# Two transformer blocks on one core: GpSimd instead of VectorE multiplies the banded attention's probabilities by the inverse sums

## The reference

```python
# 8 query heads of 64 in 2 groups of 4; blocks of 128 queries, each against its own and the previous 128 keys
scores = einsum('bnqhgd,bnkhd->bnhgqk', qb, kb) / sqrt(64)
scores = where(mask, scores, -inf)                 # distance in 0..127
m = maximum(max(scores), sink)
p = exp(scores - m)
denom = sum(p) + exp(sink - m)
out = einsum('bnhgqk,bnkhd->bnqhgd', p / denom, vb)
```

## Time and profile before

| | us |
|---|---|
| median of three runs | 2773.33 (2773.2 to 2775.22) |
| the profiled execution's own time | 2773.03 |
| its span, first to last instruction | 2771.2 |
| PE busy in the span | 2693.5 (97%) |
| DVE, ACT, POOL busy | 1417.8, 899.5, 1480.3 |
| the window part: first scores to first tile of the `w_out` product | 407.91 to 473.70 |

### The profile page before, as it was taken

The page is one execution under the profiler, slowest core; times in us unless marked ns, Lnnn a source line. Parts: engine busy times, 40 slices in busy tenths (PEclk is TensorE's granted clock), DMA queues, the critical chain, the costliest instruction groups (busy, mean ns, idle before and its releaser), DMA issues.

```text
span 2771.2 us, 34189 instructions
## 1 busy us (share of the span) xinstructions
PE 2693.5 (97%) x13446; PEld 2204.7 (80%) x13446; DVE 1417.8 (51%) x1911; ACT 899.5 (32%) x1418; POOL 1480.3 (53%) x1410
## 2 busy tenths in 40 slices
PE   7999997999999999999999999999997999999998
PEld 6989885878888888888797777878665888888887
DVE  4365638385554531835204444447678667665122
ACT  5354427242221220312113333325464222223032
POOL 3731310667777777875332221356224788786873
PEclk9999999999999999999999999999998999999999
DMA  6432330522222254435544232533021222226442
GB/s 215 167 122 84 114 120 11 182 89 65 91 92 85 83 205 175 151 92 111 120 112 94 83 111 81 190 116 107 31 76 46 76 86 81 92 77 228 152 150 101
DMA packets 184598, 309.40 MB, mean 112 GB/s; under 512 B 7044, under 2 KB 117999, under 8 KB 184439
## 3 DMA queue, kind: packets, MB, share of 16 engines
q1 hardware_dynamic: 137728, 214.45, 24.4%
q10 hardware_dynamic: 46711, 92.77, 9.5%
HBM read 232.18 MB, written 75.01 MB: 111 GB/s over the span
## 4 chain that ended last, share of the span: by engine, by line
PE 84%; DVE 9%; ACT 2%; issue 2%; POOL 2%; ACTq 0%; DMA 0%; DVEq 0%; POOLq 0%
PE PS L1039 27%; PE PS L291 20%; PE PS L1053 16%; PE PS L1724 4%; PE PS L2794 3%; PE PS L1730 2%; PE PS L1781 2%; PE PS L2428 2%; PE PS L2470 1%; PE PS L2498 1%; PE PS L2486 1%; DVE SC L658 1%; DVE XTf L1277 1%; DVE SC L2242 1%; POOL WL L3498 1%
## 5 line engine op out<-in xcount | busy, mean ns | idle before, releaser
L3494 POOL CAST WH<-raw 128x512 fp32r<-128x512 f32 (+1 forms) x240 | 180.3, 765 | 921.4 <-issue 734.3
L291 PE MATMUL PS<-UH,WH 128*128 128x512 f32 x1040 | 425.3, 409 | 8.6 <-DVE UL L739 3.7
L291 PE MATMUL PS<-UH,WL 128*128 128x512 f32 x1040 | 406.4, 391 | 0.0
L291 PE MATMUL PS<-UL,WH 128*128 128x512 f32 x1040 | 406.1, 391 | 0.0
L3498 POOL TENSOR_TENSOR WL<-raw,WH 128x512 fp32r<-128x512 f32 (+1 forms) x240 | 336.4, 1412 | 0.0
L1039 PE MATMUL PS<-UH,WH 128*128 128x512 f32 x640 | 251.4, 393 | 18.9 <-DVE SC L1307 11.3
L1593 POOL TENSOR_TENSOR WL<-raw,WH 128x512 fp32r<-128x512 f32 x176 | 259.9, 1486 | 0.0
L291 PEld LDWEIGHTS PS<-UH,WH 128*128 128x128 f32 x1040 | 195.5, 188 | 71.0 <-issue 19.8
L1039 PE MATMUL PS<-UL,WH 128*128 128x512 f32 x640 | 250.9, 392 | 0.0
L1039 PE MATMUL PS<-UH,WL 128*128 128x512 f32 x640 | 250.9, 392 | 0.0
L1558 POOL CAST WH<-WLf 128x512 fp32r<-128x512 f32 x152 | 140.4, 923 | 181.8 <-DVE WLf L1269 181.8
(11 more groups left out here) (400 smaller groups left out, 5900.7 us busy)
## 6 DMA issues: line engine op xcount, KB each, us to landing
raw<-in_w_down SPq DMA_DIRECT2D x44, 1024.0 KB, 5.7
raw<-in_w_up SPq DMA_DIRECT2D x33, 1024.0 KB, 5.1
raw<-in_w_in SPq DMA_DIRECT2D x27, 1024.0 KB, 9.8
act_rows<-SC SPq DMA_DIRECT2D x22, 1024.0 KB, 4.0
ULf<-act_rows SPq DMA_DIRECT2D x28, 512.0 KB, 3.4
raw<-in_w_gate SPq DMA_DIRECT2D x11, 1024.0 KB, 5.3
raw<-in_w_out SPq DMA_DIRECT2D x8, 1024.0 KB, 6.2
xres<-XTf ACTq DMA_DIRECT2D x16, 512.0 KB, 2.8
```

The costliest lines, as they stand in the source:

```text
L291: mm = pe.matmul(PS[:, banks[f], :], w[:, k, f * P:(f + 1) * P], u[:, k, half(h)], start=(k == 0 and j == 0), stop=(k == n_k - 1 and j == 2))
L3494: pool.tensor_copy(wh[slot][:, cols], raw[slot % 2][:, cols]).then_inc(hi_done[slot], 1)
```

## The change

The four multiplies of `divide(u)` leave DVE's queue and go to GpSimd's, in a new method `gpsimd` of the stage. GpSimd runs it for all 16 units, between the first and the second round of the segment `out1_a`. It waits for the reciprocal of the unit, multiplies, and raises a new semaphore `divided`. PE's `turn(u)` waits for that one. ACT's `probs(u)` waits, from the third unit on, until unit u - 2 is divided, since both use the same columns for their sums. What stays on DVE in `divide` is the addition and the reciprocal.

```diff
@@ setup @@
-                self.mx, self.inv, self.p_ready = c("attend_mx", 16), c("attend_inv", 32), c("attend_den", 32)
+                self.mx, self.inv, self.den_ready = c("attend_mx", 16), c("attend_inv", 32), c("attend_den", 16)
+                self.divided = c("first_divided", 16)
@@ PE, turn(u) @@
-                    pe.wait_ge(*self.p_ready(2 * u + 2))
+                    pe.wait_ge(*self.divided(u + 1))
@@ ACT, probs(u) @@
                     act.wait_ge(*self.m_ready(u + 1))
+                    if u >= 2:
+                        act.wait_ge(*self.divided(u - 1))
@@ First @@
+            def gpsimd(self, pool):
+
+                for u in range(16):
+                    nk, den = self.window_keys(u % 8)[1], self.columns(3, u)
+                    pool.wait_ge(*self.inv(2 * u + 3 if u < 15 else 32))
+                    for i in range(4):
+                        x = self.wP[u % 3][:, i * CH:i * CH + nk * P]
+                        d = pool.tensor_scalar(x, x, den[:, i:i + 1], None, ALU.mult)
+                    d.then_inc(self.divided.sem, 1)
@@ DVE, divide(u) @@
-                    nk = self.window_keys(u % 8)[1]
                     es, den = self.columns(2, u), self.columns(3, u)
                     dve.wait_ge(*self.e_done(u + 1))
-                    dve.tensor_tensor(den, den, es, ALU.add).then_inc(self.p_ready.sem, 1)
-                    dve.wait_ge(*self.p_ready(2 * u + 1))
+                    dve.tensor_tensor(den, den, es, ALU.add).then_inc(self.den_ready.sem, 1)
+                    dve.wait_ge(*self.den_ready(u + 1))
                     dve.reciprocal(den, den).then_inc(self.inv.sem, 1)
-                    dve.wait_ge(*self.inv(2 * u + 3 if u < 15 else 32))
-                    for i in range(4):
-                        x = self.wP[u % 3][:, i * CH:i * CH + nk * P]
-                        d = dve.tensor_scalar(x, x, den[:, i:i + 1], None, ALU.mult)
-                    d.then_inc(self.p_ready.sem, 1)
@@ GpSimd, the list of segments @@
                 body(0, first=True)
+                if seg == "out1_a":
+                    first.gpsimd(pool)
                 if iters > 1:
```

## The result

| | before | after |
|---|---|---|
| median, us | 2774.48 (2773.2 to 2776.11, 6 runs) | 2792.58 (2785.69 to 2794.05, 6 runs) |
| profiled execution, its span | 2773.03, 2771.2 | 2792.58, 2790.8 |
| first scores to first tile of the `w_out` product | 65.8 (407.9 to 473.7) | 83.4 (411.1 to 494.5) |
| from there to the end of the span | 2297.5 | 2296.3 |

The changed kernel is slower by 0.61% (ratio 1.0061, 95% interval 1.0048 to 1.0074), 18.1 us between the medians. The profiled spans differ by 19.6: 3.2 arise before the window part, 17.6 in it, and 1.2 are given back after it. The 3.2 are not put down to the change: the first scores began anywhere from 406.0 to 411.1 us in the fourteen profiles of this study, all of which run the same work up to there.

What follows compares the result with a forecast made beforehand. DVE was taken as the bound, ACT close second. 13 units at 3.35 us, plus 4.0 for ACT's copies, less 0.6, made 47.0 against 51.74; 4.8 - 0.7 - 0.5 = 3.6 gained, so 2769.7 us, range 2765.5 to 2778.5.

Steps and rivals of the forecast that it cites:

- What bounds the kernel now: Window part: PE waits 15.4 us for DVE's multiply; DVE sets 3.56 us per unit, ACT next with 3.26.
- What leaves DVE: DVE's queue: four multiplies, 1.06 us per full unit, leave; its pitch falls from 3.56 to about 2.4, ACT next.
- What GpSimd pays: GpSimd's queue: 0.40 us per 128 x 256 multiply, range 0.27 to 0.69; four take 1.60, so GpSimd is no bound.
- The loop of two units: Exponentials, reciprocal, multiplies, turn, copy, exponentials of unit u + 2: 6.70 us for two units, 3.35 each.
- 30 us for each microsecond on one multiply: Price sensitivity: 13 x 2 on the loop plus 4 on turn(1); the gain is gone from 0.52 us.
- its rival: GpSimd's multiply is dear: at 0.9 us each, 11.4 us worse, about 2785; chance beyond 0.70: 0.15.
- the sum: Turn(1) to turn(14): 47.0 us against 51.74, 4.8 less; minus 0.7 for a later turn(1) and 0.5 for contention: 3.6.
- The clock: PE's clock drops cost up to 1.3 and 1.0 us; without them and multiply at 0.35, gain 7.4; chance 0.25 over 5.5.
- Contention: DVE's five two-input operations beside GpSimd's multiplies each lose about 0.55 us, mostly hidden: minus 0.5 in all.
- Edits at no cost: ACT's new wait for unit u - 2 ends before it is reached; PE's wait only changes its releaser; renamed semaphores do nothing.
- The rival beyond 0.70 us: GpSimd's multiply costs over 0.70 us, making the kernel slower by more than 0.2%; chance 0.15.
- the prediction's own signs of being wrong: Four multiplies over 2.1 us, PE waiting over 15.4 us before turns, or changed time after the next product's first tile.

Runs made afterwards that it cites:

- e11: Kernel before, all multiplies on DVE, with a deeper pipeline (one turn of the loop later) and last values issued one tile earlier: 2777.4 us, ratio 1.0012.
- e5: Changed kernel with GpSimd copying each tile onto itself instead of multiplying, division left out: 2773.4 us, ratio 0.9996.
- e1: Changed kernel with GpSimd multiplying only the first 128 of the 256 columns of each tile: 2775.8 us, ratio 1.0009.
- e6: Changed kernel with half of the columns multiplied and eight added transposes on PE before each turn: 2778.9 us, ratio 1.0011.
- e3: Changed kernel with eight added transposes on PE before each turn, full width: 2787.1 us, ratio 1.0045.
- e7: Changed kernel with a fourth probabilities buffer and everything behind the exponentials one turn of the loop later: 2781.3 us, ratio 1.0023.
- e4: Kernel before, with GpSimd also doing 64 multiplies on a buffer nobody uses and nobody waiting for them: 2784.0 us, ratio 1.0037.
- e8: Changed kernel with the fourth buffer and deeper pipeline, two of four tiles multiplied on GpSimd and two on DVE: 2779.6 us, ratio 1.0013.

## Why the prediction was wrong

**What bounds the kernel now** was right. DVE's queue set the pace (e11: depth gives nothing), and what happened in the window part went through to the end, the rest changing by 1.2 us.

**What leaves DVE** was right as work: DVE's busy time in the window part fell from 59.4 to 43.7 us, about 1 us per unit. That its pitch would fall to 2.4 us, with ACT next, was not: DVE then waited for PE's scores. Even with a cheap copy in place of the multiply the pitch on the loop is 3.47 us (e5).

**What GpSimd pays** is the step that failed first. The prediction took 0.40 us per multiply of 128 x 256, near the cast, and 0.69 as the upper end; measured were 0.90. The line through the cast rows was right for a copy (0.35) and did not carry over: from 128 to 256 columns the multiply adds 0.32 us, 2.5 ns per column, more than the subtraction with two tensor inputs, for which the prediction had about 2.1. "Reads one tensor, so it is near the cast" was the wrong ground. The Trainium skill (GPSIMD Engine Reference, When to use GPSIMD), with one-input work roughly at line rate, misled in the same direction; DVE's multiply starts every 0.27 us and GpSimd's every 0.90.

**The loop of two units** was right in kind: there is one, and the length of the multiply lies on it (e1, e6). The prediction's 30 us for each microsecond on one multiply makes 15 us of the missing 0.50, so 2785 us, as its rival said. But the path was the wrong one, and this is the second step that failed. It assumed that DVE is free when the exponentials end; the loop found in the trace runs through PE's and DVE's queues, over the scores and maxima, with 5.5 instead of 5.1 us besides the multiplies; some 2.6 us more over 13 units. Its effect is seen where the price was right: in e5 the sum promised 5.1 us and the medians gave 1.3.

**The clock** was on the wrong side. The prediction let PE wait less and get its full clock back. With the dear multiply PE waited more, the granted clock fell to 0.84, and 5.5 us or more went there (e3). From 2769.7, 15.0 for the price, 2.6 for the path and 5.5 for the clock make 2792.8; the median is 2792.6. That this comes so close is luck: the same sum holds 4.0 us for ACT's copies, which don't lie on the chain of the changed kernel, and nothing for GpSimd's stretched multiplies, which do.

**Contention** fell on the other engine. The five two-input operations of DVE beside the multiplies took 1.19 to 1.42 us, where they had taken 1.22; the longest:

```profile
475.18 1.42 DVE L2303 TENSOR_TENSOR UL<-ULf,UH 128x1024 fp32r<-128x1024 f32 x1
```

That is under the 0.55 per operation that was charged. GpSimd, which was charged nothing, lost more: the four multiplies beside this one took 4.15 instead of 3.62 us, and the groups beside the other four 0.5 to 0.9 more than alone, 3.3 us in all, of which about 1.6 lie on the chain. The costly collision, of two multiplies, the change removes itself.

**Edits at no cost**: ACT's new wait never shows in the waits, and GpSimd's splits started on time.

The range was too narrow because its upper end rested on a row of another operation. The rival beyond 0.70 us named the mechanism and had 0.15. Two of the prediction's own signs of being wrong came true: four multiplies took 3.62 us, over 2.1, and PE waited 24.9 us before its turns, over 15.4. Two small slips changed nothing: 51.74 less 47.0 is 4.7, not 4.8, and the lower end of the range, 2765.5, is the sum with the multiply at DVE's pace alone (2765.8); with the clock's 2.3 us it would be 2763.5.

## What to carry to other kernels

For an operation that an engine has never run in the trace, the rows of other operations give no safe upper price: a copy at 0.35 us and a multiply at 0.90 on the same tile differ by 2.6 times. Before work is moved to a slower engine, look for the loops that it lies on, by their distance in units: the same dear multiplies cost 18 us in a loop over two units and about 6.5 us when that loop spans three (e7). Then read which queues the loop runs through: here the order in which PE and DVE issue their work closed it, and not the chain of data alone. An engine that waits more may also run slower: part of the loss here was PE at 1.2 GHz in the short stretches that were on the loop.

## What was not expected of the hardware

- GpSimd's multiply by a column, fp32: 0.58 us from start to start for 128 x 128, 0.90 for 128 x 256; by a constant about 0.82 for the latter, its copy 0.35.
- Beside GpSimd's multiplies DVE's went from 0.35 to 0.50 us, while four of GpSimd's went only from 3.62 to 3.74. Beside a two-input operation of DVE it was the other way round: 4.79 for GpSimd's four, and 1.21 for DVE's operation, as before (e4).
- The first scores began between 406.0 and 411.1 us in the profiles of these kernels, with granted clocks from 0.93 (the change, 411.1) to 1.00 (e8, 406.0) in the first 100 us. What sets this at the start of the program was not tried.
